# A decoder trunk on one Trainium2 core: the FFN down-projection rewritten as Strassen's scheme, with its block sums made by adding DMAs

## The reference

```python
def conv_ffn(x, hist, g, w_up, cw, cb, w_down):
    h = rms_norm(x, g)                      # D = 1024
    u = h @ w_up                            # 2 * F, F = 2816 = 22 blocks of 128
    c = cb + sum(cw[j] * ext[:, j:j + T] for j in range(3))   # ext: history, then u
    a, b = jnp.split(c, 2, axis=-1)
    return (jax.nn.silu(a) * b) @ w_down, ext[:, -2:]
```

## Time and profile before

| | |
|---|---|
| three runs | 2335.85, 2333.59, 2328.34 us, median 2333.59 |
| the profiled execution | 2330.3 us, of which 2328.5 us is the span from the first to the last instruction |
| mean granted TensorE clock | 0.977 of full speed |
| PE / DVE / ACT / POOL busy | 96% / 66% / 42% / 10% |
| up stages | 80 to 558 us, and 1585 to 2061 us |
| down stages | 558 to 813 us, and 2061 to 2324 us |

### The profile page before, as it was taken

The page is one execution under the profiler, slowest core; times in us unless marked ns, Lnnn a source line. Parts: engine busy times, 40 slices in busy tenths (PEclk is TensorE's granted clock), DMA queues, the critical chain, the costliest instruction groups (busy, mean ns, idle before and its releaser), DMA issues.

```text
span 2328.5 us, 46067 instructions
## 1 busy us (share of the span) xinstructions
PE 2240.7 (96%) x17352; PEld 2186.1 (94%) x17363; DVE 1543.4 (66%) x2401; ACT 989.5 (42%) x1870; POOL 228.4 (10%) x329
## 2 busy tenths in 40 slices
PE   7899999999999999999999998879999999999999
PEld 7899999998999999999999886578999999989999
DVE  5778888887455566364462776566888888864445
ACT  5544445455344433132231543354554444543333
POOL 1000000000011045152341220010000000000000
PEclk8899999999999999999999999898999999999999
DMA  6122222224654622322222796531222222255555
GB/s 197 64 65 81 81 73 72 81 83 166 243 171 142 216 80 79 97 85 92 72 82 93 238 295 184 172 132 55 65 80 81 81 78 75 87 218 198 189 185 161
DMA packets 204887, 290.39 MB, mean 125 GB/s; under 512 B 14343, under 2 KB 145719, under 8 KB 204498
## 3 DMA queue, kind: packets, MB, share of 16 engines
q1 hardware_dynamic: 199970, 284.00, 37.4%
q10 hardware_dynamic: 4792, 4.68, 0.6%
HBM read 226.64 MB, written 69.72 MB: 127 GB/s over the span
## 4 chain that ended last, share of the span: by engine, by line
PE 88%; DVE 5%; DMA 2%; ACT 2%; issue 1%; SPq 0%; ACTq 0%; POOL 0%; DVEq 0%; POOLq 0%
PE ps L1200 37%; PE ps L1289 20%; PE ps L1885 6%; PE ps L1883 6%; PE ps L1884 6%; PE ps L394 3%; PE ps L2121 2%; PE ps L2094 1%; PE ps L2105 1%; PE ps L2061 1%; PE ps L2133 1%; PE ps L826 1%; PE ps L452 1%; DMA om<-os_ 1%; PE ps L1880 1%
## 5 line engine op out<-in xcount | busy, mean ns | idle before, releaser
L1200 PE MATMUL ps<-hT,w 128*128 128x258 f32 x2752 | 462.9, 285 | 3.7 <-DVE w L1042 2.3
L1200 PEld LDWEIGHTS ps<-hT,w 128*128 128x128 f32 x2752 | 388.8, 192 | 4.6 <-DVE w L1042 2.7
L1289 PE MATMUL ps<-gdh,whl 128*128 128x384 f32 (+1 forms) x1472 | 351.3, 320 | 0.7 <-DVE x L1499 0.7
L1200 PE MATMUL ps<-lT,w 128*128 128x258 f32 x1376 | 278.8, 284 | 0.0
L1289 PEld LDWEIGHTS ps<-gdh,whl 128*128 128x128 f32 x1472 | 255.6, 189 | 1.7 <-DVE x L1499 1.3
L1200 PE MATMUL ps<-hB,w 128*128 128x258 f32 x1344 | 230.8, 284 | 4.4 <-DVE ub L1399 4.4
L1289 PE MATMUL ps<-gdl,whl 128*128 128x384 f32 (+1 forms) x736 | 234.3, 318 | 0.0
L1200 PEld LDWEIGHTS ps<-lT,w 128*128 128x128 f32 x1376 | 215.7, 192 | 0.0
L1200 PEld LDWEIGHTS ps<-hB,w 128*128 128x128 f32 x1344 | 192.0, 191 | 4.8 <-DVE ub L1399 4.8
L1151 ACT ACTIVATE w<-sq 128x1024 fp32r<-128x1024 f32 x84 | 88.8, 1057 | 174.4 <-PE ps L1200 169.6
L1479 DVE TENSOR_TENSOR whl<-stage,whl 128x1024 fp32r<-128x1024 f32 x62 | 75.9, 1224 | 108.5 <-ACT whl L1488 108.5
(11 more groups left out here) (345 smaller groups left out, 5384.3 us busy)
## 6 DMA issues: line engine op xcount, KB each, us to landing
stage<-in_w_down SPq DMA_DIRECT2D x100, 512.0 KB, 3.6
stage<-in_w_up SPq DMA_DIRECT2D x176, 256.0 KB, 3.1
gs<-cb SPq DMA_DIRECT2D x44, 516.0 KB, 2.7
graw<-gs SPq DMA_DIRECT2D x80, 192.0 KB, 3.8
rb<-in_w_down SPq DMA_DIRECT2D x30, 512.0 KB, 3.6
stage<-in_w_kv SPq DMA_DIRECT2D x24, 512.0 KB, 4.0
kvs<-kn SPq DMA_DIRECT2D x48, 256.0 KB, 2.0
xsp<-x SPq DMA_DIRECT2D x16, 516.0 KB, 2.7
```

Of the source, the lines that this page charges most:

```text
L1200: mm = pe.matmul(ps[:, bank + c, 0:HB], w, m[:, c * HB:(c + 1) * HB], start=(first and i == 0), stop=(i == len(parts) - 1), skip_group_che ...
L1289: mm = pe.matmul(ps[:, d, 0:n], wt_, m, start=(f == 0 and i == 0), stop=(f == NF - 1 and i == 2))
```

## The change

What it does:

- `THIRDS` goes. The down product becomes seven block products (`PRODUCTS` P1, P6, P7, P4, P5, P3, P2) of half the features of F (11 steps p each), half of D and half of the tokens. A step n (0 to 76) is 4 tiles d x 3 matmuls x 2 column halves of 128x258; each tile has two PSUM banks. Three of the products start PSUM afresh (`FRESH`), the others add onto the product before. After each product DVE adds or subtracts all four tiles (128x516 each) into a quadrant of x (`TARGETS`), and PE's next product waits tile by tile for that (`free`).
- A step's operands are loaded as 256 KB of weights and 264 KB of g, or of block sums. The sums are made in DRAM by POOL: `pool_sums` issues 176 DMAs a layer in 25 rounds, half copies and half adding DMAs (`accum_op`), each of 256 or 264 KB. Round `it` waits for the stores of g_it and for all DMAs of the round before. Rounds 0 to 21 fall in the up stage. DMAs in rounds 0 to 24: 4, 7, 8, 9, 10, six times 11, 9, 7, 7, 7, 6, six times 5, 3, 2, 1.
- For the differences ACT also writes a negated half of each g_f (`negated`, 128x516) and SP stores it (264 KB) to `gneg`; `f_kept` counts both stores. SP's loads for P6 and P4 wait for the rounds that make their sums (`sums_in`).
- ACT copies the last two convolution tails out before the last silu, not after it; PE begins with 36 matmuls of steps 0 and 1 ahead of them.
- The loops of the down stage are unrolled. In layer 0 the split of x goes by quadrants, spread over later steps; in layer 1 results leave after products 3, 5 and 6.

```diff
+        PRODUCTS = ("P1", "P6", "P7", "P4", "P5", "P3", "P2")
+        NP = NF // 2
+        NSTEPS = 7 * NP
+        FRESH = (0, 4, 6)
+        TARGETS = ((0, 1), (0, 0), (1, 0), (1, 1), (1, 0), (0, 0), (0, 1))
...
+        def sp_down(sp, L, S, n):
...
+            if n >= 4:
+                sp.wait_ge(f_dl, S.dl + 2 * n - 6)
...
+            if i in (1, 3):
+                sp.wait_ge(sums_in, summed(L, NP + p + (1 if i == 1 else 3)))
+            sp.dma_start(dwr[slot], wsrc).then_inc(f_wd_in[n % 4], 16)
...
+            sp.dma_start(dxr[slot], xsrc).then_inc(f_wd_in[n % 4], 16)
...
             def keep(f):
                 sp.wait_ge(f_prod, f + (S.prod + 1))
                 sp.dma_start(gs[L, bass.ds(f, 1)].rearrange("o p n -> p (o n)"), cb[:, :]).then_inc(f_kept, 16)
...
+                sp.wait_ge(f_silu_ng, 2 * f + (S.silu + 2))
+                sp.dma_start(gneg[L, bass.ds(f, 1)].rearrange("o p n -> p (o n)"), gn[:, :]).then_inc(f_kept, 16)
...
         def pe_down(pe, L, S):
...
+            def one(n, d, last):
+                i, p, slot = n // NP, n % NP, slot_of(n)
+                cols = slice(d * P, (d + 1) * P)
+                for j, (w, m) in enumerate(three(dwh[slot][:, cols], dwl[slot][:, cols], dxh[slot], dxl[slot])):
+                    for c in range(2):
+                        mm = pe.matmul(ps[:, 2 * d + c, 0:HB], w, m[:, c * HB:(c + 1) * HB],
+                                       start=(i in FRESH and p == 0 and j == 0), stop=(last and j == 2), skip_group_check=True)
                 return mm
...
+            def free(i, d):
+                if i:
+                    pe.wait_ge(f_xa, S.xa + KH * (i - 1) + d + 1)
...
+        def pool_sums(q, L, S):
+            w = a["w_down"][L]
...
+            def copy(dst, src):
+                q.dma_start(dst, src).then_inc(sums_in, 16)
...
+            def add(dst, src):
+                q.dma_start(dst, src, accum_op=ALU.add, max_dma_last_dim=4 * N).then_inc(sums_in, 16)
...
+            for it in range(SUM_ROUNDS):
+                if it < NF:
+                    q.wait_ge(f_kept, S.kept + 32 * (it + 1))
+                if it or L:
+                    q.wait_ge(sums_in, summed(L, it - 1))
...
+                    if lag == 0:
+                        copy(s1, a1[:, AL])
+                        copy(s3, a1[:, AH])
+                    elif lag == 1:
+                        add(s1, a2[:, AL])
+                        add(s3, a1[:, AL])
+                    elif lag == 2:
+                        copy(s2, s1)
...
+            def negated(f, h):
+                act.wait_ge(f_prod, f + (S.prod + 1))
+                nc.scalar.activation(gn[:, :], half(cb, h), ACT.Copy, scale=-1.0).then_inc(f_silu_ng, 1)
...
             tap(f, 1)
+            act_conv_tails(act, L, S, TAILS[NF, 0])
             silu(f)
-            act_conv_tails(act, L, S, TAILS[NF, 0])
+            negated(f, 1)
```

More of the change, by code:

```diff
@@ new lines, in step, with last_two @@
+                for d in range(KH):
+                    if p == 0:
+                        free(i, d)
+                    mm = one(n, d, p == NP - 1)
+                    if p == NP - 1:
+                        mm.then_inc(f_fin, 1)
+                if p < NP - 1:
+                    mm.then_inc(f_dn, 1)
+            def last_two(i):
+                n = NP * i + NP - 2
+                ready(n)
+                ready(n + 1)
+                for d in range(KH):
+                    one(n, d, False)
+                    one(n + 1, d, True).then_inc(f_fin, 1)
@@ L1345, in pe_down @@
                     if L == 1 and d >= 2:
-                        pe_result(pe, c, d - 2)
+                        pe_result(pe, RESULT_AT[i], d - 2)
                 if L == 1:
-                    for d in range(KC - 2, KC):
-                        pe_result(pe, c, d)
+                    for d in range(2, KH):
+                        pe_result(pe, RESULT_AT[i], d)
+            ready(0)
+            for d in range(3):
+                free(0, d)
+                one(0, d, False)
+            ready(1)
@@ L1351, in build @@
+            for d in range(3):
+                one(1, d, False)
+            pe_conv_tails(pe, S, TAILS[NF, 0])
+            free(0, 3)
+            one(0, 3, False).then_inc(f_dn, 1)
+            one(1, 3, False).then_inc(f_dn, 1)
+            for i in range(7):
+                for p in range(2 if i == 0 else 0, NP - 2 if paired(L, i) else NP):
+                    step(NP * i + p)
+                if paired(L, i):
+                    last_two(i)
         TAILS = {(NF - 3, 0): (0, 1), (NF - 3, 1): (2, 3), (NF - 2, 0): (6, 7), (NF - 2, 1): (8, 9), (NF - 1, 0): (4,),
@@ new lines, in act_split_quad @@
+        def act_split_quad(act, S, Sx, i, d):
+            j = KH * QUADS[i] + d
+            act.wait_ge(f_xa, S.xa + KH * i + d + 1)
+            if j == 0:
+                act.wait_ge(f_cs, S.cs + 2 * NF)
+            if j >= 2 and added(j - 2):
+                act.wait_ge(split_acc, Sx.acc + added(j - 2))
+            to = acc if j in (0, 4) else sq[:, d % 2, 0:N]
+            nc.scalar.activation(half(to, TARGETS[i][1]), quadrant(x, i, d), ACT.Square).then_inc(split_sq, 1)
+            nc.scalar.activation(quadrant(xh, i, d), quadrant(x, i, d), ACT.Copy).then_inc(split_hi, 1)
@@ L2559, in _ @@
             pool_start(g)
-            pool_thirds(g, split[1])
+            pool_sums(g, 0, ffn[0])
+            pool_quads(g, split[1])
             pool_project(g)
@@ L2568, in _ @@
             act_ffn(act, 0, ffn[0])
[L2570 to L2577 removed]
+            act_downs(act, ffn[0])
+            first_pieces(act, True)
+            for d in range(KH):
+                act_split_quad(act, ffn[0], split[1], 6, d)
             act_project(act)
```

588 lines of the change are left out of this document (313 added, 275 removed).

## The result

| | before | after |
|---|---|---|
| median of four runs each | 2334.7 us | 2394.2 us (2389.8 to 2398.6) |
| the profiled execution | 2330.3 us, span 2328.5 | 2390.9 us, span 2389.1 |
| ratio, with its 95% interval | | 1.0258 (1.0226 to 1.0291) |

The change makes the kernel 2.6% slower, where 2.1% faster was forecast; 2394 lies far outside 2270 to 2322. The page of after, to be read beside the earlier trace rows: PE's busy share fell from 96% to 93%, POOL now works, and a DMA queue has appeared that was not there.

What follows compares the result with a forecast made beforehand. PE was taken to bound the kernel. The terms 50.4 + 6.6 - 3 - 2 - 4 gave 48 us saved, 2282.3 or 2285.6 us; 2284 was named, its own range 2270 to 2298, 8 in 10 runs 2270 to 2322.

Steps and rivals of the forecast that it cites:

- PE's own work: Down stage: 77 steps at 120.0 ns a matmul take 221.8 us, not 247.0; 25.2 us less per layer, 50.4 for two.
- The opening: Down stage's start: earlier tail copies save 1.7 us of PE's wait and 1.6 of half clock, 6.6 us over both layers.
- Product boundaries: Six per layer in the down stage: 0.2 us lost at ten, 0.9 at two of layer 1; net cost 3 us.
- The ends: Layer 0 to projection 0, at most 2 us either way; layer 1's end 2 us more, 1 to 4.
- Casts hidden, ACT's negation and second store free: Down-stage casts and subtractions hide under PE's 2.88 us step; up-stage negation and second store fit existing waits, no cost.
- Beside the up stage: POOL's summing DMAs run during the up stage; weight loads land in 7.7 us, inside a limit of 8; cost 4 us.
- Rival 1: Up stage: the round's DMAs delay weight loads by 3.5 us in each of 20 heavy f's, 70 us, 2352; 22%.
- Rival 2: Sums are late for P6's loads, 66 us in each layer if POOL needs 3.1 us per DMA, 2414 us; 8%.

Runs made afterwards that it cites:

- e1: Changed kernel without POOL's rounds: no sums made, equally large blocks of w_down and g loaded instead; 2284.9 us, ratio 0.9782 to the kernel before.
- e5: Kernel before, with only ACT's copies of the last two tails moved ahead of the last silu; ratio 0.9970, 7.0 us less.
- e2: Changed kernel with each adding DMA made a plain copy of the same bytes, so sums are not made; 2318.1 us, ratio 0.9929.
- e8: Changed kernel with POOL's transfers in pieces of at most 1024 bytes; 2336.1 us, ratio 0.9997 to the kernel before.
- e11: As e9, but rounds 21 to 24 wait until step 12 of the down stage is done; 2307.1 us, ratio 0.9891.
- e4: Changed kernel with POOL's transfers cut into 128-byte pieces; 4187.1 us, ratio 1.7919 to the kernel before.
- e9: As e7, with rounds 21 to 24 also waiting until PE has finished step 7 of the down stage; 2304.9 us, ratio 0.9871.
- e7: Changed kernel with weight sums started two in three rounds, each round waiting until the part-1 weight loads have landed; 2309.5 us, ratio 0.9902.
- e13: Changed kernel with POOL's transfers in pieces of at most 2064 bytes; 2400.8 us, ratio 1.0287 to the kernel before.
- e10: As e9, with POOL's transfers in pieces of at most 1024 bytes; 2364.7 us, ratio 1.0111 to the kernel before.

## Why the prediction was wrong, point by point

- **PE's own work: right.** 25.2 us less a layer were counted. ACT's casts stand 2.89 us apart (714.55 and 717.44 us in after's timeline); 77 steps of it are 222.5 us, for 221.8 counted. In e1 the down stages are 29.0 and 28.4 us shorter than before, the opening's 3.3 included.
- **The opening: right.** 6.6 us counted, 7.0 measured alone (e5); PE's wait is 1.5 us in each layer, no half clock behind it, and PE does not wait for step 4.
- **Product boundaries: right in size.** In layer 0 the profile shows PE idle at none of them but the first, which is the loss of the down stage's beginning. In layer 1 it idles 1.0 and 1.1 us at the two where it also transposes the last tile, put at 0.9.
- **The ends: 2 us short.** From layer 0 to the projection PE waits 5.8 us, for 6.0 before. From the last down matmul to the end of the span it is 8.9 us, for 5.0 before: 3.9 more, where 2 was counted.
- **Casts hidden, ACT's negation and second store free: right.** e1's up stages are within 0.1 us of before's.
- **Beside the up stage: this step failed.** "I put 4 us for both layers"; it is 95, and some 18 in the down stages (236.6 and 242.5 us for e1's 226.3 and 234.6) that no term held. Three sizes in it were wrong. First the length of a round: 10.8 us were counted, "if its five adds read their target as well", and 13.5 came. An adding packet takes a little over twice a copying one, 178 ns for 84 in 2 KB (329 for 160 in 4128 bytes), more than a second read at the engines' full rate; in e2, without adding, 76 of 109 us are gone. Second the head start: "at most 4.6 us of the round's 10.8 can stand before them" grants the round 6.2 us ahead of the loads. POOL's first issue does come 5.9 us before them (309.97 and 315.9), but its first packet moves only at 311.2, so the round had 4.7. What stood before the loads was 13.5 - 4.7 = 8.8 us, not 4.6, and the second load landed after 10.8 us (316.5 to 327.3), not 7.7. The form of the estimate was right, and it was called inside a limit of 8 by 0.3 us, so its two inputs should have had a range that reached across. Third the price of being over the limit: 10.8 is 2.8 over 8, and PE's gap is 2.8, but the half clock after it, 1.6 us, was left out, although the same prediction had counted it at the tails. Over both up stages the gaps make 63 us and the half clock 27, for 95 measured in all.
- **Rival 1 (22%, of which 12 for a part of it that still left a gain) is what happened, and in full**: f's of 21.8 to 26.4 us in rounds 1 to 11 of layer 0, with DVE's weight sum waiting for `stage`, as its sign was described. Its price, 3.5 us for each of 20 f's or 70 us, lacks the half clock too and still was the nearest of all terms to the 95. Its arithmetic, 64 packets times 0.132 us, was not the reason, though, and that the price came near was partly luck: the packet-by-packet turns that the Trainium skill describes (page "DMA: Bandwidth & Descriptors", section "Queues, rings and completion order") are in the traces, at 77 packets a microsecond here and 120 in e8, but most of a pair's packets pass as the round runs out. Its point of decision, a landing of 8 us, was right: 10.8 loses, 3.3 (e1) does not, and the 9.3 to 10.4 of e2 lose 1.2 to 2.3 us.
- **Rival 2 (sums late): no** in the changed kernel, where SP waits for no sums in the down stages. In e11, where rounds 21 and 22 were pushed back, and in e4 it came true.
- **Not in any case**: that the last rounds meet the catching-up loads in the down stage's opening. There the engines were at 0.84 already; what is queued in that stretch should have been gone through for each DMA that the change adds. Nor do rounds 0 to 21 all fall in the up stage, as the description of the change has it: in layer 0 POOL issues round 20 at 606.9 us, 1.5 us before the down stage's first matmul, and round 21 at 623.7, within it.

The gain that was counted is there to within 3.3 us when the rounds are not (e1: 2284.9 for 2281.6). The changed kernel gives it away twice over through DMAs that PE never waits for directly. With the rounds even, behind the loads, and the last ones after step 7 (e9), the kernel makes all its sums and takes 2304.9 us, 1.3% less than before and 89 us less than the change as it was made. e9 and e7 can't be told apart for sure (their intervals overlap).

## What to carry to other kernels

Work put on idle DMA engines is not free because the engines have room on average: ask of each load with little slack which burst can stand in front of it, and let the burst start when that load has landed, not when its own inputs are ready. An adding DMA is to be priced at twice a copy, and a burst by its whole length, since here a load of many small packets beside it landed only when it had ended. When the burst is moved, look at once at who meets it next (here the stores), and shorten it until nobody does.

## What the runs showed of the hardware that was not expected

- A DRAM-to-DRAM adding DMA took 178 ns (median) for a 2 KB packet and 329 for 4128 bytes, where a load of 2 KB takes 84 and a copy of 4128 bytes 160. In pieces of 1 KB it took 102 ns, of 128 bytes 36: a fixed part of about 26 ns and 0.074 ns a byte (from 128 bytes and 2 KB; the line gives 102 at 1 KB).
- Two queues shared the engines about one packet each: 77 weight packets a microsecond beside 178-ns pieces, 120 beside 102-ns pieces.
- POOL issues 11 DMAs in 7.4 us (309.97 to 317.3), well ahead of the engines; within some rounds its issues stopped, for 4.3 us in e8 and 2.6 in e13.
- Many small pieces cost more than their bytes: adding pieces of 1 KB took 60 us more where the rounds already stood behind the loads. Over layer 0's up stage POOL's packets kept the 16 engines only about a tenth longer (215 us for 199); why it costs so much is open. In e10's trace several heavy rounds last 16 to 23 us and run into the next.
- Half clock did not follow every gap of PE. In layer 0's up stage it came with eight gaps of 2.0 to 4.8 us and not with three of 1.1, 3.1 and 3.2, and in e2's layer 0 with none of seven gaps of 1.2 to 2.3.
